# One pack set less on TensorE, and products of two conv tiles added by accumulating transfers

## The chip, the core and the metric

The kernel runs on one core of a Trainium2 chip. Its metric is the device time of one execution in microseconds; before the change three runs gave 802.43, 802.77 and 803.06 us, median 802.77. A core has four engines that compute, each with its own instruction stream: TensorE (PE, matmuls, with its weight loads shown as PEld), VectorE (DVE), ScalarE (ACT) and GpSimd (POOL). SyncE (SP) issues transfers. The engines meet only at semaphores.

## The reference

Two decoder layers over 512 positions of width 1024 in float32: a Conformer convolution layer, then latent attention. The change is in the first one:

```python
proj = h @ w_in + b_in                       # 512 x 1024 @ 1024 x 6144
val, glu_gate, z = jnp.split(proj, 3, axis=-1)
u = val * jax.nn.sigmoid(glu_gate)           # 512 x 2048
u = causal depthwise conv(u, conv_w, 31 taps per channel) + conv_b
u = jax.nn.silu(layer_norm(u, norm_g, norm_b))
return (u * jax.nn.silu(z)) @ w_out + b_out
```

The layer norm is over all 2048 channels, so the mean needs every channel's convolution.

## The kernel before

**Tiles and chunks.** Channels lie on the partitions: the 2048 channels are 16 tiles of 128 partitions x 512 positions. The input projection goes by chunks of 128 output columns: chunks 0 to 31 alternate value and gate (pair t is chunks 2t and 2t+1 and gives tile t of u), chunks 32 to 47 give the 16 tiles of z (z0 to z15). For accuracy a float32 product is three matmuls of high and low parts: with 8 row blocks a chunk is 24 matmuls. For each chunk SyncE loads the weights (w_raw, 512 KB), ScalarE writes the high part (w_hi, L1013), GpSimd the low part (w_lo, L820, a "split"), and TensorE multiplies. There are two buffers of w_raw and four of w_hi and w_lo.

**Pair t on ScalarE** (`value_gate`, L1039): w_hi of both chunks, then val of tile t-1 (waits for TensorE to finish chunk 2t-2), products "before gating", starts of VectorE chains, then the sigmoid of tile t-1 (waits for chunk 2t-1), products "after gating", further starts. On GpSimd (`value_gate`, L835): two splits, product additions, u of tile t-1 (val times sig, L832), more.

**The convolution** is done in three ways.
- *VectorE tiles* (`convolve`, L1518): 12 tiles in the order of VECTOR_TILES, each as two chains of multiply-add in two PSUM banks (L1470), then joined (L1496). ScalarE starts a tile by writing its first taps to the banks (`start_chains`, L1059); where it does so is in the START tables. The last one, LATE_TILE, has its first 17 taps summed elsewhere and 14 here.
- *Shared tiles*: ScalarE multiplies u by one tap into a ring of four buffers (`tap_times_u`, L1083), GpSimd adds it (L860). These are all taps of tile 1 and the first 17 of tile 11.
- *Matrix tiles* 4, 8 and 12 (`pack`, L1941): u is written to DRAM, read back shifted (`stacked`), and four packs of six matmuls follow four chunks of the projection (from PACKS_AT). ScalarE keeps each pack's result, SyncE moves its parts (`move_parts`), and VectorE adds three of them (`add_parts`, L1499).

**After that** VectorE and GpSimd add all 16 tiles to csum; TensorE sums csum over partitions inside chunk z11 (`sum_over_channels`, L1980), VectorE centres the tiles, the squares are summed in z14, and the projection of the branch follows. Every engine's order is written out in the program; the tables below set where each piece stands.

Of the kernel before, what the change touches and what calls it, by code (L numbers as in the profile page):

```python
# [122 lines left out]
def trunk_kernel(nc, x, positions, ln_g, ln_b, a_w_in, a_b_in, a_conv_w, a_conv_b, a_norm_g,  # L123
# [14 lines left out]
    with ExitStack() as ctx:  # L138
# [388 lines left out]

        def pair_taps(t):

            first = sum(n for at_pair, n in PAIR_SHARE.items() if at_pair < t)  # L530
            return range(first, first + PAIR_SHARE.get(t, 0))

        def z_taps(i):

            first = sum(PAIR_SHARE.values()) + sum(n for at_chunk, n in Z_SHARE.items() if at_chunk < i)
# [1731 lines left out]
```

## Time and profile before

| what | value |
|---|---|
| median of three runs | 802.77 us (802.43 to 803.06) |
| the profiled execution | 800.57 us |
| its span, first to last instruction | 798.8 us |
| TensorE busy | 786.2 us, 98% |
| VectorE busy | 587.5 us, 74% |
| GpSimd busy | 527.9 us, 66% |
| ScalarE busy | 392.3 us, 49% |
| granted TensorE clock | 0.999 |

A busy share is an average over stages with different limits: VectorE's 74% hides a stretch of some 240 us in which it never rests. Matmuls overlap in the pipeline, so their busy times add up to more than they cost; the interval from one to the next is what counts. Line numbers in rows are those of the kernel before.

### The profile page before, as it was taken

The numbers are of one execution on the slowest core, as the hardware profiler recorded it, in microseconds if no ns is written. First come the engines' busy times: TensorE is split into PE (matmuls) and PEld (weight loads), VectorE is DVE, ScalarE is ACT, GpSimd is POOL, SyncE is SP. The second block draws the span as 40 slices with busy tenths as digits, with TensorE's granted clock in tenths as the row PEclk, the third lists the DMA queues.
The fourth block names the chain that finished last, engine by engine and source line by source line (L and its number), as shares of the span: only waits on it lengthen the run. The fifth ranks groups of instructions, "written<-read, shape, count | busy, mean of one in ns | idle before, by whom it ended". The sixth has DMA issues, their size and how long they took to land.

```text
span 798.8 us, 11166 instructions
## 1 busy us (share of the span) xinstructions
PE 786.2 (98%) x3811; PEld 664.6 (83%) x3811; DVE 587.5 (74%) x1000; ACT 392.3 (49%) x687; POOL 527.9 (66%) x324
## 2 busy tenths in 40 slices
PE   7999999999999999999999999999999999999996
PEld 7888888888888878888988788889888888888885
DVE  3699999999999869975633490059788988877217
ACT  4555554653734577521433453157676766655110
POOL 4589997996997763862564457247768667367430
PEclk9999999999999999999999999999999999999999
DMA  6333476564653325632333225236666664653412
GB/s 226 106 106 92 129 193 176 133 189 139 157 141 109 103 80 163 208 122 62 106 106 118 80 79 172 66 106 181 188 186 202 191 204 134 197 181 130 158 54 105
DMA packets 130030, 111.35 MB, mean 139 GB/s; under 512 B 16986, under 2 KB 109248, under 8 KB 129980
## 3 DMA queue, kind: packets, MB, share of 16 engines
q1 hardware_dynamic: 129980, 110.72, 47.1%
q8 instruction: 27, 0.44, 0.2%
q14 instruction: 23, 0.19, 0.1%
HBM read 88.85 MB, written 14.25 MB: 129 GB/s over the span
## 4 chain that ended last, share of the span: by engine, by line
PE 86%; POOL 6%; issue 4%; DMA 2%; DVE 0%; SPq 0%; ACT 0%; DVEq 0%; POOLq 0%
PE bank L1867 81%; POOL w_lo L820 5%; PE bank L2180 1%; PE bank L2181 1%; DMA x_in<-in_x_dram 1%; POOL res L936 1%; PE bank L1957 1%; PE bank L1954 1%; PE bank L1955 1%; POOL vsum_odd L885 1%; DMA w_raw<-in_a_w_out_dram 1%; PE bank L2054 0%; PE bank L2173 0%; PE bank L2171 0%; PE bank L2107 0%
## 5 line engine op out<-in xcount | busy, mean ns | idle before, releaser
L820 POOL TENSOR_TENSOR w_lo<-w_raw,w_hi 128x1024 fp32r<-128x1024 f32 x102 | 253.7, 2496 | 122.7 <-ACT w_hi L1013 115.2
L1470 DVE SCALAR_TENSOR_TENSOR bank<-u,conv_w,bank 128x512 f32<-128x512 f32 x291 | 193.6, 748 | 0.0
L1013 ACT ACTIVATE w_hi<-w_raw 128x1024 fp32r<-128x1024 f32 x102 | 107.4, 1057 | 105.5 <-DMA w_raw<-in_a_w_in_dram 43.0
L1867 PE MATMUL bank<-xt_hi,w_lo 128*128 128x512 f32 (+1 forms) x392 | 152.1, 388 | 0.0
L1867 PE MATMUL bank<-xt_hi,w_hi 128*128 128x512 f32 (+1 forms) x392 | 150.9, 385 | 0.0
L1867 PE MATMUL bank<-xt_lo,w_hi 128*128 128x512 f32 (+1 forms) x392 | 150.9, 385 | 0.0
L1867 PEld LDWEIGHTS bank<-xt_lo,w_hi 128*128 128x128 f32 x392 | 73.7, 188 | 15.1 <-issue 0.5
L1867 PEld LDWEIGHTS bank<-xt_hi,w_lo 128*128 128x128 f32 x392 | 73.7, 188 | 15.0 <-issue 0.5
L1867 PEld LDWEIGHTS bank<-xt_hi,w_hi 128*128 128x128 f32 x392 | 73.6, 188 | 14.9
L1867 PE MATMUL bank<-ht_hi,w_lo 128*128 128x512 f32 (+1 forms) x208 | 76.4, 367 | 0.0
L1867 PE MATMUL bank<-ht_lo,w_hi 128*128 128x512 f32 (+1 forms) x208 | 75.8, 365 | 0.0
L1867 PE MATMUL bank<-ht_hi,w_hi 128*128 128x512 f32 (+1 forms) x208 | 75.8, 365 | 0.0
L972 POOL TENSOR_TENSOR pt_lo<-prob_moved,pt_hi 128x512 fp32r<-128x512 f32 (+1 forms) x64 | 55.9, 906 | 17.8 <-ACT pt_hi L1342 17.8
L941 POOL TENSOR_TENSOR bundle_lo<-bundle_raw,bundle_hi 128x1024 fp32r<-128x1024 f32 (+1 forms) x16 | 49.2, 3074 | 27.1 <-ACT bundle_hi L1269 27.1
L860 POOL TENSOR_TENSOR acc<-acc,tap_product 128x512 f32<-128x512 f32 x46 | 59.6, 1296 | 4.1 <-ACT tap_product L1093 0.8
L1867 PE MATMUL bank<-w_hi,fg_lo 128*128 128x512 f32 x128 | 50.1, 391 | 0.7 <-issue 0.7
L1867 PE MATMUL bank<-w_hi,g_lo 128*128 128x512 f32 x128 | 50.2, 392 | 0.6 <-POOL w_lo L820 0.3
L1867 PE MATMUL bank<-w_hi,g_hi 128*128 128x512 f32 x128 | 49.9, 389 | 0.0
L1867 PE MATMUL bank<-w_hi,fg_hi 128*128 128x512 f32 x128 | 49.8, 389 | 0.0
L1867 PE MATMUL bank<-w_lo,fg_hi 128*128 128x512 f32 x128 | 49.8, 389 | 0.0
L1867 PE MATMUL bank<-w_lo,g_hi 128*128 128x512 f32 x128 | 49.8, 389 | 0.0
L1643 DVE SCALAR_TENSOR_TENSOR bank<-res,bank 128x512 f32<-128x512 f32 x16 | 11.0, 689 | 50.4 <-PE bank L1867 50.4
(225 smaller groups left out, 1730.4 us busy)
## 6 DMA issues: line engine op xcount, KB each, us to landing
w_raw<-in_a_w_in_dram SPq DMA_DIRECT2D x48, 512.0 KB, 3.8
w_raw<-in_b_w_in_dram SPq DMA_DIRECT2D x20, 512.0 KB, 3.7
prob_kept<-prob SPq DMA_DIRECT2D x16, 640.0 KB, 3.5
prob_moved<-prob_kept SPq DMA_DIRECT2D x64, 160.0 KB, 3.2
w_raw<-in_a_w_out_dram SPq DMA_DIRECT2D x16, 512.0 KB, 4.0
w_raw<-in_b_w_out_dram SPq DMA_DIRECT2D x16, 512.0 KB, 3.6
stacked<-u_kept SPq DMA_DIRECT2D x48, 132.0 KB, 4.1
bundle_raw<-in_b_w_uq_dram SPq DMA_DIRECT2D x16, 256.0 KB, 4.5
```

The source lines that it names most:

```text
L820: nc.gpsimd.tensor_tensor(w_lo[slot][:], w_raw[raw][:], w_hi[slot][:].bitcast(F32), ALU.subtract).then_inc(w_lo_ready, 1)
L860: nc.gpsimd.tensor_tensor(acc[:, t, :], acc[:, t, :], tap_product[n % 4][:], ALU.add).then_inc(product_added, 1)
L885: nc.gpsimd.tensor_tensor(vsum_odd[:], vsum_odd[:], sq[t % 4][:], ALU.add).then_inc(vsum_odd_done, 1)
L936: nc.gpsimd.tensor_tensor(res[:, r, :], res[:, r, :], ln_rows[:, 2, :], ALU.add).then_inc(res_ready, 1)
L941: nc.gpsimd.tensor_tensor(bundle_lo[slot][part][:], bundle_raw[:, lo:hi], bundle_hi[slot][part][:].bitcast(F32), ALU.subtract).then_inc(bu ...
L972: nc.gpsimd.tensor_tensor(turned_block(pt_lo, b), moved_block(b), turned_block(pt_hi, b).bitcast(F32), ALU.subtract).then_inc(pt_lo_ready, 1)
L1013: nc.scalar.activation(w_hi[slot][:], w_raw[raw][:], ACT.Copy).then_inc(w_hi_ready, 1)
L1470: nc.vector.scalar_tensor_tensor(out=inner[:] if k < TAPS - 1 else acc[:, t, :], in0=u[:, t, k:k + SEQ], scalar=conv_w[:, column:column + ...
L1643: nc.vector.scalar_tensor_tensor(out=total[:], in0=rows_half, scalar=scale, in1=total[:], op0=ALU.mult, op1=ALU.add).then_inc(y_step, 1)
L1867: last = nc.tensor.matmul(out_ap, a, b, start=(start and n == 0 and m == 0), stop=(stop and n == len(parts) - 1 and m == 2))
L1954: nc.tensor.matmul(out[:], matrix_lo[:, g, s, :], stacked[:, 0, g, window], start=s == 0, stop=False)
L1955: nc.tensor.matmul(out[:], matrix_hi[:, g, s, :], stacked[:, 0, g, window], start=False, stop=False)
```

## The change

The tiles are dealt out anew. Matrix tiles are 8 and 12; tile 4 leaves them. BEGINS goes from (6, 10, 14) to (10, 14), PACKS_AT from (17, 25, 35) to (26, 35). Tile 4 becomes the late tile, with 22 taps summed by ScalarE and GpSimd and 9 on VectorE; tile 11 becomes a full VectorE tile and tile 7 a shared one. Most products of tiles 1 and 7 are no longer added one at a time. ScalarE writes four of them side by side (four tiles' width, in parts of acc and z_a that are free then), and GpSimd issues one transfer that adds these 128 x 2048 values to four running sums. There are 11 such transfers; then GpSimd adds the four sums to one. Tile 1 has 7 groups of four (the first is written as the sums) and 3 single taps, tile 7 has 6 groups and 7 single taps. VectorE waits for six and for ten groups before the last tap of tiles 9 and 13, whose places in acc the groups use; ScalarE waits for all 11 before z1.

```diff
-        MATRIX_ROWS = (1, 2, 3)
+        MATRIX_ROWS = (2, 3)
-        BEGINS = (6, 10, 14)
-        PACKS_AT = (17, 25, 35)
+        BEGINS = (10, 14)
+        PACKS_AT = (26, 35)
-        LATE_TILE, LATE_TAPS = 11, 17
-        SHARED_TILES = (1,)
-        VECTOR_TILES = (0, 2, 3, 5, 6, 7, 9, 10, 13, 14, 15, LATE_TILE)
-        PAIR_SHARE = {3: 3, 4: 4, 5: 2, 6: 3, 7: 4, 8: 3, 9: 4, 10: 3, 11: 1, 12: 4, 13: 4, 14: 3, 15: 1}
-        Z_SHARE = {0: 1, 1: 2, 2: 2, 3: 2, 4: 2}
+        GROUPED_TILES = (1, 7)
+        LATE_TILE, LATE_TAPS = 4, 22
+        VECTOR_TILES = (0, 2, 3, 5, 6, 9, 10, 11, 13, 14, 15, LATE_TILE)
+        GROUP = 4
+        FIRST_GROUPS, SECOND_GROUPS = 6, 5
+        GROUP_PAIRS = (4, 5, 6, 7, 8, 9, 11, 12, 13, 14, 15)
...
+        for t, n in ((6, 3), (7, 2), (8, 2), (9, 3), (12, 3), (13, 4), (14, 2), (15, 1)):
+            AFTER_GATING[t] = taps_of(LATE_TILE, first, n)
+            first += n
+        IN_Z[1] = taps_of(LATE_TILE, first, LATE_TAPS - first)
+        first = GROUPED_TAPS[1]
+        for i, n in ((3, 2), (4, 2), (5, 2), (6, 1)):
+            IN_Z[i] = taps_of(LATER, first, n)
+            first += n
...
-        PARTS_AFTER = {7: 0, 13: 1, LATE_TILE: 2}
+        PARTS_AFTER = {13: 0, LATE_TILE: 1}
-        START_BEFORE_GATING = {5: 3, 7: 5, 10: 7, 15: 13}
-        START_AFTER_GATING = {3: 2, 8: 6, 11: 9, 13: 10}
-        START_IN_Z = {1: 14, 7: 15, 10: LATE_TILE}
+        START_BEFORE_GATING = {5: 3, 7: 5, 11: 9, 12: 10, 14: 11, 15: 13}
+        START_AFTER_GATING = {3: 2, 8: 6}
+        START_IN_Z = {3: 14, 7: 15, 10: LATE_TILE}
...
+                if t == GROUP_PAIRS[FIRST_GROUPS]:
+                    sum_group(0)
+                if t == GROUP_PAIRS[FIRST_GROUPS] + 1:
+                    add_products(BEFORE_GATING[10])
+                add_products(AFTER_GATING.get(t - 1, ()))
                 if t > 0:
                     glu(t - 1, (t - 1) % 2)
+                if t in GROUP_PAIRS:
+                    add_group(GROUP_PAIRS.index(t))
...
+            def add_group(g):
+
+                t, k = BEFORE_GATING[GROUP_PAIRS[g]][-1]
+                pool.wait_ge(product_ready, shared_taps.index((t, k)) + 1)
+                wait(pool, group_added, 16 * g)
+                nc.gpsimd.dma_start(group_sums(t)[:], group_products(g)[:], accum_op=ALU.add).then_inc(group_added, 16)
+
+            def sum_group(which):
+
+                t = GROUPED_TILES[which]
+                pool.wait_ge(group_added, 16 * (FIRST_GROUPS + which * SECOND_GROUPS))
+                for n in range(1, GROUP):
...
+                elif apart(t, k):
+                    g = k // GROUP - 1 + FIRST_GROUPS * GROUPED_TILES.index(t)
+                    wait(act, group_added, 16 * (g - 1))
+                    if g == 7:
+                        act.wait_ge(group_summed, GROUP - 1)
+                    out = group_products(g)[:, k % GROUP, :]
...
+                if i == 1:
+                    act.wait_ge(group_added, 16 * len(GROUP_PAIRS))
...
+                    if t in (9, 13) and k == TAPS - 1:
+                        dve.wait_ge(group_added, 16 * (FIRST_GROUPS if t == 9 else 10))
```

Three places show how this moves instructions. The first is GpSimd in pair 14 and the start of pair 15; L820 (before) and L858 (after) are splits, L832 and L870 write u. Before:

```order
L820 TENSOR_TENSOR w_lo0_77<-w_raw0_71,w_hi0_73 128x1024
L820 TENSOR_TENSOR w_lo1_78<-w_raw1_72,w_hi1_74 128x1024
L860 TENSOR_TENSOR acc_105<-acc_105,tap_product3_120 128x512
L860 TENSOR_TENSOR acc_105<-acc_105,tap_product0_117 128x512
L860 TENSOR_TENSOR acc_105<-acc_105,tap_product1_118 128x512
L832 TENSOR_TENSOR u_95<-val1_83,sig1_85 128x512
L877 TENSOR_TENSOR u_lo_96<-u_95,cu_hi_86 128x542
L820 TENSOR_TENSOR w_lo2_79<-w_raw0_71,w_hi2_75 128x1024
L820 TENSOR_TENSOR w_lo3_80<-w_raw1_72,w_hi3_76 128x1024
L860 TENSOR_TENSOR acc_105<-acc_105,tap_product2_119 128x512
```

The same stretch on GpSimd after the change:

```order
L858 TENSOR_TENSOR w_lo0_77<-w_raw0_71,w_hi0_73 128x1024
L858 TENSOR_TENSOR w_lo1_78<-w_raw1_72,w_hi1_74 128x1024
L920 TENSOR_TENSOR acc_106<-acc_106,tap_product0_118 128x512
L920 TENSOR_TENSOR acc_106<-acc_106,tap_product1_119 128x512
L920 TENSOR_TENSOR acc_106<-acc_106,tap_product2_120 128x512
L920 TENSOR_TENSOR acc_106<-acc_106,tap_product3_121 128x512
L870 TENSOR_TENSOR u_95<-val1_83,sig1_85 128x512
L899 DMA second_sums_97<-acc_106 128x2048
L937 TENSOR_TENSOR u_lo_96<-u_95,cu_hi_86 128x542
L858 TENSOR_TENSOR w_lo2_79<-w_raw0_71,w_hi2_75 128x1024
L858 TENSOR_TENSOR w_lo3_80<-w_raw1_72,w_hi3_76 128x1024
L920 TENSOR_TENSOR acc_106<-acc_106,tap_product0_118 128x512
```

This pair has one addition more, all ahead of u, and the transfer stands between u and u_lo.

The second place is ScalarE where it starts VectorE's sixth tile, in banks 3 and 7. Before, this is pair 10 and tile 7:

```order
L1013 ACTIVATE w_hi0_73<-w_raw0_71 128x1024
L1036 ACTIVATE part_out0_108<-bank6 128x512
L1013 ACTIVATE w_hi1_74<-w_raw1_72 128x1024
L1019 ACTIVATE val1_83<-bank0,vec_51 128x512
L1093 ACTIVATE tap_product3_120<-u_95,conv_w_62 128x512
L1093 ACTIVATE tap_product0_117<-u_95,conv_w_62 128x512
L1093 ACTIVATE tap_product1_118<-u_95,conv_w_62 128x512
L1069 ACTIVATE bank3<-u_95,vec_51,conv_w_62 128x512
L1072 ACTIVATE bank7<-u_95,conv_w_62 128x512
```

After the change it is tile 9, from the end of pair 10 into pair 11:

```order
L1176 ACTIVATE cu_hi_86<-u_95 128x542
L1169 ACTIVATE second_sums_97<-u_95,vec_51,conv_w_62 128x512
L1171 ACTIVATE second_sums_97<-u_95,conv_w_62 128x512 x3
L1077 ACTIVATE w_hi2_75<-w_raw0_71 128x1024
L1077 ACTIVATE w_hi3_76<-w_raw1_72 128x1024
L1083 ACTIVATE val0_82<-bank2,vec_51 128x512
L1171 ACTIVATE z_a_111<-u_95,conv_w_62 128x512 x4
L1131 ACTIVATE bank3<-u_95,vec_51,conv_w_62 128x512
L1134 ACTIVATE bank7<-u_95,conv_w_62 128x512
```

The start of the sixth tile has moved back by one pair, behind the val of tile 10 and four products.

The third place is VectorE from the late tile to csum. Before:

```order
L1481 SCALAR_TENSOR_TENSOR bank<-u,conv_w,acc 128x512
L1470 SCALAR_TENSOR_TENSOR bank<-u,conv_w,bank 128x512 x10
L1470 SCALAR_TENSOR_TENSOR acc<-u,conv_w,bank 128x512
L1470 SCALAR_TENSOR_TENSOR bank<-u,conv_w,bank 128x512
L1496 TENSOR_TENSOR acc<-bank,acc 128x512
L1507 TENSOR_TENSOR bank<-u,bank 128x508
```

VectorE at the same place after the change:

```order
L1562 SCALAR_TENSOR_TENSOR bank<-u,conv_w,acc 128x512
L1551 SCALAR_TENSOR_TENSOR bank<-u,conv_w,bank 128x512 x4
L1551 SCALAR_TENSOR_TENSOR acc<-u,conv_w,bank 128x512
L1551 SCALAR_TENSOR_TENSOR bank<-u,conv_w,bank 128x512 x2
L1577 TENSOR_TENSOR acc<-bank,acc 128x512
L1588 TENSOR_TENSOR bank<-u,bank 128x508
```

Five multiply-adds are gone, and the last two of the first chain now follow each other.

## Rows read from the trace of the kernel before

**Rows 1.** The page, part 1: busy time of each engine.
```profile
PE 786.2 (98%) x3811; PEld 664.6 (83%) x3811; DVE 587.5 (74%) x1000; ACT 392.3 (49%) x687; POOL 527.9 (66%) x324
```
**Rows 2.** Waits of PE: who waited, for whom, us in total, times, longest.
```profile
PE bank L1885 <- DMA x_in<-in_x_dram: 2.7, 3, 2.4
...
PE bank L1867 <- POOL w_lo L820: 0.3, 1, 0.3
PE bank L1867 <- DVE g_lo L1595: 0.2, 1, 0.2
```
**Rows 3.** The chain that ended last: start us, us, what.
```profile
168.67 5.45 PE bank L1867 x24
175.52 5.45 PE bank L1867 x24
...
221.85 5.44 PE bank L1867 x24
```
**Rows 4.** Timeline at the mean: start us, us, engine, line, operation.
```profile
263.41 0.68 DVE L1507 TENSOR_TENSOR bank<-u,bank 128x508 f32<-128x508 f32 x1
...
265.46 0.69 DVE L1456 COPY bank<-acc 128x512 f32<-128x512 f32 x1
...
267.05 0.69 DVE L1458 TENSOR_TENSOR csum<-bank,pool_csum 128x512 f32<-128x512 f32 x1
...
267.86 0.39 PEld L1983 LDWEIGHTS bank<-csum,ones 128*128 128x128 f32 x2
```
**Rows 5.** Stretches: busy us of PE, PEld, DVE, ACT, POOL; clock, DMA share, GB/s.
```profile
30.00:90.00 60.00, 60.00 (x266) 49.66 (x265) 59.74 (x94) 32.60 (x49) 53.31 (x32) 1.00 0.36 106
90.00:150.00 60.00, 60.00 (x266) 49.56 (x265) 59.90 (x91) 33.11 (x48) 53.89 (x34) 1.00 0.58 159
```
**Rows 6.** Timeline of DVE: the fifth and sixth tile, and the late tile's first tap.
```profile
110.37 17.86 DVE L1470 SCALAR_TENSOR_TENSOR bank<-u,conv_w,bank 128x512 f32<-128x512 f32 x27
...
130.20 17.87 DVE L1470 SCALAR_TENSOR_TENSOR bank<-u,conv_w,bank 128x512 f32<-128x512 f32 x27
...
253.25 1.62 DVE L1481 SCALAR_TENSOR_TENSOR bank<-u,conv_w,acc 128x512 f32<-128x512 f32 x1
```
**Rows 7.** Timeline of ACT in pairs 6 to 12.
```profile
78.76 0.69 ACT L1025 ACTIVATE sig<-bank,vec 128x512 f32<-128x512 f32 x1 [2.86 <-PE bank L1867]
79.34 0.65 ACT L1099 ACTIVATE cu_hi<-u 128x542 fp32r<-128x542 f32 x1
...
84.84 2.55 ACT L1093 ACTIVATE tap_product<-u,conv_w 128x512 f32<-128x512 f32 x4
87.30 0.77 ACT L1069 ACTIVATE bank<-u,vec,conv_w 128x512 f32<-128x512 f32 x1
...
100.52 0.69 ACT L1025 ACTIVATE sig<-bank,vec 128x512 f32<-128x512 f32 x1 [2.85 <-PE bank L1867]
...
140.66 2.00 ACT L1013 ACTIVATE w_hi<-w_raw 128x1024 fp32r<-128x1024 f32 x2
```
**Rows 8.** Timeline of POOL in pairs 11, 12, 14, 15 and at z3.
```profile
111.42 4.18 POOL L860 TENSOR_TENSOR acc<-acc,tap_product 128x512 f32<-128x512 f32 x3
115.56 1.29 POOL L832 TENSOR_TENSOR u<-val,sig 128x512 f32<-128x512 f32 x1
...
128.18 1.38 POOL L877 TENSOR_TENSOR u_lo<-u,cu_hi 128x542 fp32r<-128x542 f32 x1
...
177.51 4.75 POOL L820 TENSOR_TENSOR w_lo<-w_raw,w_hi 128x1024 fp32r<-128x1024 f32 x2
...
189.89 1.99 POOL L871 TENSOR_TENSOR matrix_hi<-same_channel,stack_hi 128x1024 fp32r<-128x1024 f32 x1
...
210.42 2.42 POOL L820 TENSOR_TENSOR w_lo<-w_raw,w_hi 128x1024 fp32r<-128x1024 f32 x1
```
**Rows 9.** One more stretch, columns as in rows 5.
```profile
150.00:207.00 57.00, 57.00 (x253) 47.07 (x252) 56.86 (x88) 31.42 (x46) 49.47 (x31) 1.00 0.64 170
```
**Rows 10.** SyncE's issue of a load (timeline), and the landing of loads (page, part 6).
```profile
231.83 0.53 SPq L566 DMA_DIRECT2D w_raw<-in_a_w_in_dram  x1
...
w_raw<-in_a_w_in_dram SPq DMA_DIRECT2D x48, 512.0 KB, 3.8
```

More of the change, by code:

```diff
@@ L419, in added_before, with taps_of @@
-        def added_before(n):
-            return sum(1 for _, k in shared_taps[:n] if k > 0)
+        GROUPED_TILES = (1, 7)
[4 more added lines that the diff above has]
+        GROUP_PAIRS = (4, 5, 6, 7, 8, 9, 11, 12, 13, 14, 15)
+        GROUPED_TAPS = (GROUP * (FIRST_GROUPS + 1), GROUP * (SECOND_GROUPS + 1))
+        def taps_of(t, first, n):
+            return [(t, k) for k in range(first, first + n)]
@@ new lines, in trunk_kernel @@
+        first = 0
+        for t, n in ((6, 3), (7, 2), (8, 2), (9, 3), (12, 3), (13, 4), (14, 2), (15, 1)):
[6 more added lines that the diff above has]
+            first += n
+        shared_taps = [tap for t in range(CT) for half in (BEFORE_GATING, AFTER_GATING) for tap in half.get(t, ())]
@@ new lines, in trunk_kernel, with apart, added, added_up_to @@
+        shared_taps += [tap for i in range(CT) for tap in IN_Z.get(i, ())]
+        def apart(t, k):
+            return t in GROUPED_TILES and k < GROUPED_TAPS[GROUPED_TILES.index(t)]
+        def added(t, k):
+            return k > 0 and not apart(t, k)
+        def added_up_to(tap):
+            return sum(1 for t, k in shared_taps[:shared_taps.index(tap) + 1] if added(t, k))
+        def group_sums(t):
+            return acc[:, CT - GROUP:, :] if t == EARLIER else second_sums
+        def group_products(g):
+            if g in (7, 9):
+                return acc[:, CT - GROUP:, :]
+            if g in (1, 3, 5):
+                return acc[:, CT - 2 * GROUP:CT - GROUP, :]
+            return z_a[:, 1:1 + GROUP, :]
@@ L526, in starts_before @@
             return 2 * STARTED.index(t) + (0 if t == LATE_TILE else slot)
[L528 to L535, printed above, removed]
-            return range(min(first, len(shared_taps)), min(first + Z_SHARE.get(i, 0), len(shared_taps)))
         LOOP_BEGINS, LOOP_ROUNDS = 3, 2
@@ new lines, in add_products @@
+            def add_products(taps):
+                for t, k in taps:
+                    if not added(t, k):
+                        continue
+                    if t in GROUPED_TILES:
+                        pool.wait_ge(group_summed, (GROUP - 1) * (GROUPED_TILES.index(t) + 1))
+                    pool.wait_ge(product_ready, shared_taps.index((t, k)) + 1)
+                    wait(pool, product_added, added_up_to((t, k)) - 1)
+                    nc.gpsimd.tensor_tensor(acc[:, t, :], acc[:, t, :], tap_product[added_up_to((t, k)) % 4][:], ALU.add
+                                            ).then_inc(product_added, 1)
@@ L910, in _ @@
                     split_lo(Z0 + 1, 1, 1)
+                    add_products(AFTER_GATING[CT - 1])
                     glu(CT - 1, (CT - 1) % 2)
-                for n in z_taps(i):
-                    add_product(n)
+                if i == 2:
+                    sum_group(1)
+                add_products(IN_Z.get(i, ()))
                 if i >= POOL_SUM_BEGINS:
@@ L1043, in value_gate @@
                 keep_value(t - 1, (t - 1) % ROUND)
-                for n in pair_taps(t)[:BEFORE_GATING + 1]:
-                    tap_times_u(n)
-                if t in PARTS_START_IN_PAIR:
-                    start_parts(PARTS_START_IN_PAIR[t])
+                for tap in BEFORE_GATING.get(t, ()):
+                    tap_times_u(*tap)
                 if t in START_BEFORE_GATING:
@@ L1053, in value_gate @@
                     conv_input_hi(BEGINS.index(t))
-                for n in pair_taps(t)[BEFORE_GATING + 1:]:
-                    tap_times_u(n)
+                for tap in AFTER_GATING.get(t, ()):
+                    tap_times_u(*tap)
                 if t in START_AFTER_GATING:
@@ L1199, in _ @@
                     square(t)
-                for n in z_taps(i):
-                    tap_times_u(n)
+                for tap in IN_Z.get(i, ()):
+                    tap_times_u(*tap)
             output_split(0)
```

79 lines of the change are left out of this document (46 added, 33 removed).

## The prediction

> **What bounds the kernel now.** I read the page first: TensorE is busy 98% of the span [rows 1]. The table of waits, filtered to TensorE, says the same from the other side: its longest in total is 2.7 us, at the start for x, and for the other engines' work it waits 0.3 and 0.2 us in the whole run [rows 2]. So any matmul that goes is worth its issue interval, as long as nobody comes late to a place where TensorE asks for something. The chain of waits gives that interval: 24 matmuls of a chunk take 5.44 us (0.227 each), and with a pack behind the chunk the next starts 6.85 us later, so a pack of six costs 1.40 us [rows 3]. Not 6 x 0.39: busy times of matmuls overlap.
>
> The next view is the timeline around the mean over channels, in chunk z11. VectorE writes csum, 267.05 to 267.74; TensorE's weight load for the sum starts at 267.86, in step with its own rhythm [rows 4]. VectorE has been busy without a gap since 30 us (59.7 of 60, 59.9 of 60) [rows 5]. At this place two engines bound the kernel together: TensorE's gain counts only as far as VectorE comes earlier too. What follows the mean (centring, variance, projection) is the same code, started by csum, so I take its length as unchanged.
>
> **The change, part by part.**
>
> *TensorE.* One pack set of three goes: 4 packs x 1.40 = 5.6 us. Without any wait TensorE would ask for csum at 267.86 - 5.6 = 262.3.
>
> *VectorE, removed.* The late tile takes 9 taps for 14, one of each begun by ScalarE. 27 taps take 17.86 us, 0.66 each [rows 6]: 5 x 0.66 = 3.3, less some 0.1 because the order now ends with two dependent taps (x2 in the listing). One set of three part additions goes: 263.41 to 265.46, 2.05 us [rows 4]. The first late tap stays at its 1.62 us [rows 6]. Together -5.25 us: csum at 262.5, nearly as early as TensorE.
>
> *VectorE, a new wait.* VectorE's sixth tile starts when ScalarE has put its first tap into the banks. Before, tile 7 was started in pair 10; now it is tile 9, in pair 11, behind four grouped products. VectorE is free at 130.20 [rows 6]; the starts of the tiles before it keep their places or have some 2 us of room. ScalarE's sigmoid of tile 5 is at 78.76 and of tile 7 at 100.52 [rows 7], which is 4 chunks x 5.44. No pack now stands behind chunks 17 to 20, so the end of chunk 20 comes at 100.52 + 5 x 5.44 = 127.7. ScalarE reaches it from the sigmoid of tile 9 (122.3) with 0.6 for that, 0.55 for cu_hi, 2.6 for the four products of tile 7, 2.0 for two w_hi [rows 7]: 128.0. Then val 0.6, four products 2.46 (84.84 to 87.30), the start 0.77: 131.8. VectorE stands still 131.8 - 130.2 = 1.6 us. It has no later slack: it never idles before csum. The other starts have room. A tile lasts 19.8 us (110.37 to 130.20) [rows 6], so VectorE wants tile 10 at 131.8 + 19.8 = 151.6; ScalarE starts it after val of tile 11 (end of chunk 22, 138.6) and 4.5 us more, at 143.1. Tile 11 is wanted at 171.4 and started near 166 (end of chunk 26, 160.4).
> csum then comes at 267.74 - 5.25 + 1.6 = 264.1, TensorE waits about 1.8 us for it, and the gain is 3.65 us, say 3.7.
>
> *GpSimd.* 46 additions become 37, and 11 accumulating transfers are issued. From pair 10 on GpSimd is the busiest after VectorE, and TensorE needs its w_lo. Intervals [rows 8]: split 2.37, addition 1.37 (three 4.14), u 1.24, u_lo 1.32, the two matrices 3.9. Let X be GpSimd's time for one transfer. If u of tile 8 waits for its sigmoid (112.1), it ends at 113.4. Then: one X; pair 10, 2 splits, 3 additions, u, u_lo 11.4; pairs 11 to 13, 10.1 + X each; pair 14 with four additions and u_lo 12.8 + X; pair 15 with two additions and the matrices 12.6 + X; split of z0 2.4. Sum 182.9 + 6X. TensorE begins z0 at 100.52 + 16 x 5.44 + 4 x 1.40 = 193.2. So GpSimd is in time up to X = 1.7. Above that, pairs 8 and 9 lose their slack too (counted from u of tile 6: sigmoid of tile 5 at 78.76, three products and a w_hi to 82.2, two splits and two additions to 89.7, the sigmoid it waits for at 90.3, done at 91.6; then 8.7 + X for each of the two pairs and their X), and z0 is late by 8X - 14.6. A lateness under 1.8 costs nothing, since TensorE would wait for csum anyway. The next tight place is z3, where three additions of tile 7's sums lie ahead: before, its split was done at 212.84 [rows 8], and z4 began at 221.85 [rows 3], so z3 at 221.85 - 1.40 - 5.44 = 215.0: 2.2 us early. With X = 1.3 I get about the same: u of tile 15 ends at 195.1, two additions, a split, three additions and a split later it is 206.8 for 209.4. From z5 on there are four additions more, but GpSimd has rest there once ScalarE waits for the last pack.
>
> What is X? No row shows a transfer issued by GpSimd. From below SyncE's issue, 0.53 us [rows 10]; from above the time in which GpSimd itself works through as many columns, two splits, 4.75 us. I take 1.3, between, nearer to SyncE's row because the instruction only names the data. At 1.3 z0 is ready 2.4 us early and the cost is 0.
> The Trainium skill ("DMA: Bandwidth & Descriptors", section on latency and other measured facts) gives about 1 us for the first byte on the GpSimd path; no run here shows it so far. By it the sum would be the same 3.7.
>
> *The transfers.* Each adds 1 MB to 1 MB in SBUF. GpSimd waits before each for the one before, issued 10.9 us or more earlier. Bounds for the landing: 3.8 us, as a 512 KB load takes [rows 10], and 11.4, three times that, since 3 MB move (two reads, a write) for 1 MB. I take 7.6, two loads' worth: no wait. The DMA engines are already busy 0.36, 0.58 and 0.64 of three stretches [rows 5, 9]; the weight loads would land later, and they have some 3.6 us of room (split to split of a slot 10.9, less split 2.4, load 3.8, w_hi 1.05).
> The Trainium skill (same page, section on issuing engines that are not separate DMA queues) says that all transfers share the same 16 engines whoever issues them. That speaks against the change; its own fit (2.0 us plus size over 436 GB/s, section on the anatomy of one DMA) gives 4.4 us as an estimate for 1 MB, and then nothing is late.
>
> *ScalarE.* 36 more products at 0.62 = 22 us in a stretch where it is busy 33 of 60 us. They delay no w_hi that GpSimd is waiting for, except through the ring of four products in pairs 13 and 14, where I see about 1 us of room. Taken as 0. The first pack in z waits for VectorE's parts of tile 8, done at 131.8 + 4 x 19.8 + 2.05 = 213.1; TensorE comes there at 215.0 - 5.6 + 5.44 = 214.8.
>
> **Sum.** -5.6 + 1.8 (wait for csum) = -3.7 us with rounding. Against the profiled execution (800.57 us, of it 798.8 span) that is 796.9; it lies 2.2 under the median of the runs, 802.77, on which I forecast 799.1.
>
> **Rivals.**
> 1. *TensorE's whole gain.* The start of tile 9 is in time, or VectorE catches up: -5.25 to -5.6, 797.3. For it: the stall rests on 1.6 us of ScalarE's order. Against: the order is fixed, and VectorE has no gap to catch up in.
> 2. *GpSimd late, but not by more than the packs were worth.* X between 2.0 and 2.5: z0 late by 1.8 to 5.4, result 799.1 to 802.6. For and against as in rival 3.
> 3. *Slower: GpSimd's issue.* w_lo of z0 is the place. From X = 2.5 the lateness passes 5.6. At X = 3, 8 x 3 - 14.6 = 9.4, less 5.6: 3.8 slower, 806.6. For it: 4.75 us is not excluded, and GpSimd works 53.9 of 60 us there [rows 5]. Against: SyncE's 0.53.
> 4. *Transfers land late.* GpSimd then stands before the next one. With landing time L, from the transfer of pair 7 at 91.6: two L to that of pair 9, 22.9 through pair 10 to that of pair 11, four L to that of pair 15, 7.6 to z0's w_lo. That is 122.1 + 6L, late from L = 11.9, slower from 12.8; at 13 the lateness is 6.9 and the result 804.1, at 14 810. For it: an upper bound of 11.4 and shared engines; against: the lower ones.
> That the set of packs doesn't go is excluded: the listing has eight packs.
>
> **Numbers.** Forecast 42%; rival 1 12%; rival 2 16% (6 faster, 10 within); rival 3 18%; rival 4 12%, both counted slower. So faster by over 0.2% (1.6 us, about what a measurement of this kernel can tell from no change) 60%, within 10%, slower 30%. The likeliest case alone spans 798.3 to 800.0. The range for 8 in 10 takes in rival 1 and about two thirds of 3 and 4: 796.8 to 806.
>
> **What the profile after would show.** Right: 16 matmuls of each pack line; VectorE idle about 1.6 us before its sixth tile, with ScalarE's start as releaser; TensorE idle near 1.8 us before the csum product and nowhere else before it; GpSimd's splits in time at z0 and z3. Wrong: TensorE waiting for w_lo in pairs 12 to 15 or z0 (X too small), GpSimd idle ahead of a transfer (landing), ScalarE waiting longer for weight loads, or no wait at csum (rival 1).

## The result: 0.39% slower

| | median | lowest to highest | profiled execution | its span |
|---|---|---|---|---|
| before | 800.77 us | 799.16 to 803.35 us, and one run of 2050.48 us | 800.57 us | 798.8 us |
| after | 803.60 us | 801.03 to 807.09 us | 802.84 us | 801.0 us |

The ratio is 1.0039, with a 95% interval from 1.0027 to 1.0052 (20 runs of each, the one of 2050.48 us left out): some 3 us slower, where 3.7 us less was forecast (799.1 on a median of 802.77, a ratio of 0.9954). The forecast was reckoned from three runs; twenty put the kernel before at 800.77. The measured time lies inside the range that was given, 796.8 to 806, on the other side of no change. The runs of after also scatter over 6 us.

**TensorE.** The table of waits of the kernel after, from 100 to 215 us (who waited, for whom, us in total, times, longest):

```profile
ACT w_hi L1077 <- DMA w_raw<-in_a_w_in_dram: 15.6, 8, 3.6
...
PE bank L2035 <- ACT part_out L1100: 4.4, 1, 4.4
DVE bank L1551 <- ACT bank L1131: 2.1, 1, 2.1
```

Before, TensorE's waits for other engines' work were 0.2 and 0.3 us in the whole run [rows 2]. Now there is one of 4.4 us at a pack's first matmul (L2035), for ScalarE's copy of the preceding pack's result (L1100). VectorE's new wait, forecast at 1.6 us, is there with 2.1. The chain that ended last, of after, says why ScalarE was late (start, us, what):

```profile
148.69 2.71 POOL w_lo L858
151.47 0.39 SPq L602
151.90 0.70 SPq L619
...
155.61 0.86 SPq L619
156.58 8.10 DMA w_raw<-in_a_w_in_dram
164.93 0.74 issue
165.67 0.67 ACT val L1083
...
166.85 1.94 ACT acc L1171 x3
168.78 0.67 ACT bank L1131
169.45 0.61 ACT bank L1134
170.07 0.53 ACT part_out L1100
170.73 0.77 PE bank L2035
...
172.77 0.85 PE bank L2038 x2
173.63 6.71 PE bank L1948 x24
```

Read from the bottom: the pack began at 170.73 because ScalarE's copy of the pack before came at 170.07; ahead of it in ScalarE's order stand a start (L1131, L1134), four grouped products and val; and val stands behind w_hi of chunk 29, whose weights took 8.1 us to land. SyncE issued that load behind four shifted reads of tile 8 (L619) that took 4.58 us to issue; in kernel 9 below, which has no transfers, they took 2.00.

The same rows hold a second cost. The late pack takes 173.63 - 170.73 = 2.90 us where 1.40 is normal, and the chunk behind it 6.71 for 5.44 [rows 3]: 2.8 us more, with nobody waiting. The stretches of after show it (busy us of PE, PEld, DVE, ACT, POOL; granted clock, DMA share, GB/s):

```profile
160.00:163.00 3.00, 3.00 (x14) 2.46 (x14) 3.00 (x6) 1.31 (x2) 2.29 (x3) 1.00 1.17 221
...
166.00:169.00 3.00, 0.35 (x2) 0.00 (x0) 3.00 (x6) 3.00 (x6) 3.00 (x2) 1.00 0.97 224
169.00:172.00 3.00, 1.27 (x3) 1.11 (x4) 2.97 (x6) 3.00 (x6) 2.71 (x3) 0.55 0.36 105
172.00:175.00 3.00, 3.00 (x8) 2.32 (x8) 3.00 (x6) 2.35 (x4) 2.86 (x4) 0.50 0.46 112
175.00:178.00 3.00, 3.00 (x12) 2.38 (x12) 3.00 (x6) 0.66 (x1) 3.00 (x3) 0.81 1.06 296
```

After TensorE had stood, the granted clock was at its lower level (0.50, 1.2 GHz) while it worked again, 8 matmuls in 3 us for 15 in the same 3 us before, and back at 1.00 behind 178.

**The mean.** Timeline of after from VectorE's last steps to csum and TensorE's product (start, us, engine, line, operation, idle time before and its releaser):

```profile
262.44 0.70 DVE L1537 TENSOR_TENSOR bank<-bank,acc 128x512 f32<-128x512 f32 x1
264.07 0.69 DVE L1537 TENSOR_TENSOR csum<-bank,pool_csum 128x512 f32<-128x512 f32 x1 [0.94 <-POOL pool_csum L965]
...
268.84 1.02 PE L2064 MATMUL bank<-csum,ones 128*128 128x512 f32 x2
```

csum was done at 264.76, where 264.1 was forecast, but TensorE came 4 us later: 268.84, before 268.06. Since its first matmul of the projection was 0.76 us earlier in after (11.03 for 11.79: x landed sooner), the sum up to here is -5.6 (packs) + 4.4 (standing) + 2.8 (clock) = +1.6, and the traces say 268.84 - 268.06 + 0.76 = +1.5. From this product to the end of the span it is 532.2 us against 530.7, +1.4 more, at the same code. In total -0.8 + 1.5 + 1.4 = 2.2 with rounding, the difference of the spans.

**The transfers.** Queues and issues, page of after, parts 3 and 6 (packets, MB, share of 16 engines; KB each, median us to landing):

```profile
q0 software_dynamic: 1584, 11.54, 7.5%
...
w_raw<-in_a_w_in_dram SPq DMA_DIRECT2D x48, 512.0 KB, 4.1
stacked<-u_kept SPq DMA_DIRECT2D x32, 132.0 KB, 6.1
acc<-z_a POOLq DMA_DIRECT2D x3, 1024.0 KB, 7.3
...
second_sums<-acc POOLq DMA_DIRECT2D x2, 1024.0 KB, 9.4
```

q0 is GpSimd's queue: 7.5% of 801 us is 60 us of all 16 engines, 5.5 us for each of eleven transfers. From 150 to 170 us the DMA share is 1.07, where before it was 0.70. A short stretch above 1 stood in before too (1.06 from 160 to 163 us); what is new is how long it lasts, 1.03 over 137 to 169 us for 0.61. The shifted reads land in 6.1 us instead of 4.1 (medians, as all landings of this table). GpSimd's issue is short, and what comes right behind it is some 0.3 us longer (two splits, 5.07 for 4.75):

```profile
137.03 0.87 POOL L899 DMA_DIRECT2D second_sums<-z_a  x1
137.64 5.07 POOL L858 TENSOR_TENSOR w_lo<-w_raw,w_hi 128x1024 fp32r<-128x1024 f32 x2
```

### The profile page after: what moved, and what is told of

Read it like the earlier page. It is cut to its first block, busy times and chain, and to the rows that moved or that the text cites. A ratio compares the mean times of both kernels' runs of the same rounds, so it can differ in the third digit from the quotient of the medians.

```text
span 801.0 us, 11092 instructions
## 1 busy us (share of the span) xinstructions
PE 784.1 (98%) x3787; PEld 662.6 (83%) x3787; DVE 575.4 (72%) x992; ACT 410.7 (51%) x717; POOL 523.6 (65%) x323
## 4 chain that ended last, share of the span: by engine, by line
PE 89%; DMA 3%; POOL 2%; SPq 2%; ACT 1%; issue 1%; DVE 1%; DVEq 0%; ACTq 0%
PE bank L1948 84%; POOL pt_lo L1036 1%; DMA w_raw<-in_a_w_in_dram 1%; DMA x_in<-in_x_dram 1%; DMA prob_kept<-prob 1%; PE bank L2261 1%; PE bank L2262 1%; POOL w_lo L858 1%; SPq L619 1%; PE bank L2035 0%; DMA prob_moved<-prob_kept 0%; PE bank L2038 0%; PE bank L2036 0%; POOL bundle_lo L1005 0%; PE bank L2135 0%
## 5 line engine op out<-in xcount | busy, mean ns | idle before, releaser
L858 POOL TENSOR_TENSOR w_lo<-w_raw,w_hi 128x1024 fp32r<-128x1024 f32 x102 | 254.1, 2513 | 127.7 <-ACT w_hi L1077 120.2
L1551 DVE SCALAR_TENSOR_TENSOR bank<-u,conv_w,bank 128x512 f32<-128x512 f32 x286 | 190.4, 748 | 2.2 <-ACT bank L1131 2.1
L1948 PE MATMUL bank<-xt_hi,w_lo 128*128 128x512 f32 (+1 forms) x392 | 152.6, 389 | 0.0
L1948 PE MATMUL bank<-xt_hi,w_hi 128*128 128x512 f32 (+1 forms) x392 | 151.4, 386 | 0.0
L1948 PE MATMUL bank<-xt_lo,w_hi 128*128 128x512 f32 (+1 forms) x392 | 151.3, 386 | 0.0
L1948 PEld LDWEIGHTS bank<-xt_hi,w_lo 128*128 128x128 f32 x392 | 74.1, 189 | 15.2 <-issue 0.5
L1948 PEld LDWEIGHTS bank<-xt_lo,w_hi 128*128 128x128 f32 x392 | 74.0, 189 | 15.2 <-issue 0.5
L1948 PEld LDWEIGHTS bank<-xt_hi,w_hi 128*128 128x128 f32 x392 | 73.9, 189 | 14.9
L1948 PE MATMUL bank<-ht_hi,w_lo 128*128 128x512 f32 (+1 forms) x208 | 76.4, 367 | 1.0 <-DVE ht_lo L1758 1.0
L1948 PE MATMUL bank<-ht_lo,w_hi 128*128 128x512 f32 (+1 forms) x208 | 75.8, 365 | 0.0
L1948 PE MATMUL bank<-ht_hi,w_hi 128*128 128x512 f32 (+1 forms) x208 | 75.8, 365 | 0.0
L1036 POOL TENSOR_TENSOR pt_lo<-prob_moved,pt_hi 128x512 fp32r<-128x512 f32 (+1 forms) x64 | 60.2, 975 | 16.3 <-ACT pt_hi L1421 16.3
L1948 PE MATMUL bank<-w_hi,fg_lo 128*128 128x512 f32 x128 | 50.1, 391 | 0.7 <-issue 0.7
L1948 PE MATMUL bank<-w_hi,g_lo 128*128 128x512 f32 x128 | 50.0, 391 | 0.2 <-DVE g_lo L1676 0.2
L1948 PE MATMUL bank<-w_hi,g_hi 128*128 128x512 f32 x128 | 49.8, 389 | 0.0
L1948 PE MATMUL bank<-w_lo,g_hi 128*128 128x512 f32 x128 | 49.8, 389 | 0.0
L1948 PE MATMUL bank<-w_hi,fg_hi 128*128 128x512 f32 x128 | 49.8, 389 | 0.0
L1948 PE MATMUL bank<-w_lo,fg_hi 128*128 128x512 f32 x128 | 49.8, 389 | 0.0
L1948 PEld LDWEIGHTS bank<-ht_hi,w_lo 128*128 128x128 f32 x208 | 39.2, 189 | 7.6 <-DVE ht_lo L1758 1.2
```

What stands on the lines that cost most here:

```text
L858: nc.gpsimd.tensor_tensor(w_lo[slot][:], w_raw[raw][:], w_hi[slot][:].bitcast(F32), ALU.subtract).then_inc(w_lo_ready, 1)
L1036: nc.gpsimd.tensor_tensor(turned_block(pt_lo, b), moved_block(b), turned_block(pt_hi, b).bitcast(F32), ALU.subtract).then_inc(pt_lo_ready, 1)
L1551: nc.vector.scalar_tensor_tensor(out=inner[:] if k < TAPS - 1 else acc[:, t, :], in0=u[:, t, k:k + SEQ], scalar=conv_w[:, column:column + ...
L1948: last = nc.tensor.matmul(out_ap, a, b, start=(start and n == 0 and m == 0), stop=(stop and n == len(parts) - 1 and m == 2))
```

## The experiments

All are the changed kernel with the edit shown, unless said otherwise; ratios are to the kernel before on the same chip, with 95% intervals.

**1. The pack's result is kept first** (`keep_first`).

```diff
                 keep_value(t - 1, (t - 1) % ROUND)
+                keep_pack_after(2 * t - 2)
                 for tap in BEFORE_GATING.get(t, ()):
                     tap_times_u(*tap)
                 if t in START_BEFORE_GATING:
                     start_chains(START_BEFORE_GATING[t])
-                keep_pack_after(2 * t - 2)
```

> The changed kernel with one thing moved: ScalarE keeps a pack's result ahead of the four products and the start of a VectorE tile, not behind them (pairs 14 and 15). Theory T: the result of the sign is one stall. TensorE waited 4.4 us at the second pack of tile 8 for ScalarE to keep the first pack's result, and its clock then fell, which cost some 3.3 us more (34 matmuls fewer than in before between 150 and 190 us, 34 x 0.227 = 7.7, of it 4.4 standing). ScalarE was late because a weight load landed late and because products and a start (4.0 us) stood ahead of the keep. With the keep first the stall is at most 0.5 us, the clock stays at 1.00, TensorE comes to the csum product at 269.0 - 7.7 = 261.3 and waits there for VectorE's csum (264.8, or 263.8 without its 0.9 us wait for GpSimd). Time some 4.2 to 5 us below the changed kernel, about 799 against 803.6, 0.2% to 0.3% under the kernel before. Rival R (the loss is spread: slower loads and GpSimd's issues everywhere, the stall is only where it shows): the stall turns up at another place, and the time stays within 1.5 us of the changed kernel, 0.2% to 0.4% over the kernel before.

Measured 1.0021 (1.0000 to 1.0042), where the change had 1.0039: 1.4 us gained, not 4.2 to 5, and the two intervals overlap. The stall at the packs went from 4.4 to 1.4 us, but TensorE reached the csum product at 268.57, hardly earlier. Its waits from 100 to 215 us:

```profile
PE bank L1948 <- issue: 2.9, 2, 1.8
PE bank L2035 <- ACT part_out L1100: 1.4, 2, 0.9
```

The chain of this kernel puts the new ones at 199.63 and 206.41, ahead of z chunks (L1948), where tile 12's shifted reads run and w_hi waited up to 6.1 us for a load; the stretches from 206 to 214 us show a clock of 0.89 and 0.68. In after, TensorE did not stand there (20.00 of 20 us busy from 190 to 210, at a DMA share of 0.98): its stall at 166 had put it behind. So T was right on the place and wrong on the cause: not one stall but a shortage, and rival R came nearer.

**2. Kept ahead of the start only** (`keep_mid`): in the diff above the line stands between the products and the start.

> The changed kernel with the keep of a pack's result moved only ahead of the start of a VectorE tile (1.4 us of the 4.0), behind the four products. Asks for the price of a stall by its length. Theory T: the stall falls from 4.4 to about 3.0 us and the clock still falls, at the same extra of about 3.3: TensorE at the csum product near 267.6, time 1.4 us below the changed kernel. Rival (the extra goes with the length of the stall): 4.4 to 3.0 takes 7.7 to 5.2, 2.5 us below.

Measured 1.0023 (1.0007 to 1.0039). TensorE stood 3.1 us. Its chain shows what that cost in clock:

```profile
169.18 0.69 PE bank L2035
...
171.15 0.85 PE bank L2038 x2
172.00 5.86 PE bank L1948 x24
```

2.82 us for the pack and 5.86 for the chunk, 1.4 + 0.4 = 1.8 us too much, against 2.8 after a stall of 4.4 us. The extra is not fixed. With 1.3 us less standing the csum product came 2.5 us earlier, at 266.37, of which 0.3 is an earlier first matmul: the expectation's rival came nearer. The medians of the runs gained 1.3 us, which the intervals do not tell from none.

**3. And tile 9 started first** (`keep_start9`): as 1, and for t == 11 the start stands ahead of the products.

> As the kernel with the keep first, and in pair 11 ScalarE starts tile 9 ahead of the four products of tile 7. Theory T: VectorE's 2.1 us wait before its sixth tile goes, csum is 1 to 2 us earlier than in the kernel with the keep first (as far as GpSimd's own sum is in time), TensorE waits less at the mean, and the time falls by another 1 to 2 us, to about 797.5, 0.4% under the kernel before. If GpSimd's sum is the later one, the gain stays under 0.5 us. Rival R: no difference, since VectorE is not what the end waits for.

Measured 1.0024 (1.0004 to 1.0044), as kernel 1. VectorE still waited 1.5 us for the start (val ahead of it was late) and 2.4 us for GpSimd's sum, and then 5.0 us for TensorE. Where TensorE is late, an earlier csum is worth nothing.

**4. Small transfers** (`small_transfers`).

```diff
-                nc.gpsimd.dma_start(group_sums(t)[:], group_products(g)[:], accum_op=ALU.add)
+                nc.gpsimd.dma_start(group_sums(t)[:, :, 0:32], group_products(g)[:, :, 0:32], accum_op=ALU.add)
```

> The changed kernel with each accumulating transfer cut to 32 of its 512 columns: the issue on GpSimd, ScalarE's products, every wait and SyncE's order stay, what the DMA engines move is a sixteenth. The other columns of the groups' sums are left out. Theory T (the DMA engines were full from 137 to 169 us and made the load late): loads land in 3.8 us as before, the stall goes from 4.4 to under 1 us, DMA share in 150 to 170 falls from 1.07 to about 0.7, the time is that of the kernel with the keep first, about 799. Rival S (SyncE's queue: the load's issue stands behind four shifted reads whatever the engines do): the load's issue still comes at about 156.6 and the stall keeps 2 us or more. Rival A (ScalarE's 22 us more of products by themselves make it late): the stall stays 3 us or more, the time within 1 us of the changed kernel.

Measured 0.9977 (0.9961 to 0.9992), 799.0 us: T's number. Stall 1.5 us at the pack, clock in 150 to 210 us 1.00, csum product at 263.57:

```profile
150.00:170.00 20.00, 18.46 (x82) 14.98 (x81) 19.96 (x32) 16.40 (x26) 19.31 (x12) 1.00 0.53 120
170.00:190.00 20.00, 20.00 (x90) 16.47 (x89) 19.96 (x31) 11.38 (x17) 19.82 (x13) 1.00 0.71 172
```

ScalarE's products, all waits and SyncE's order are the same, so what the DMA engines moved made the loss. Rival S holds for a part, though: the load of chunk 29 was still issued at 155.94 us (156.58 in after, 152.89 without any transfers), behind four reads whose issue took 3.30 us, and w_hi of that chunk began at 161.66 for 159.12 without transfers; the 1.5 us of standing come with that. Nor is GpSimd's own issue the same: it takes 1.28 us for such a cut transfer and 0.87 for a whole one. In the time none of this shows, since TensorE would have waited for csum anyway (kernel 9).

**5. Only tile 7's transfers small** (`second_small`): the same cut for g >= 6.

> As the kernel with small transfers, but only the five of tile 7 (pairs 11 to 15) are cut to 32 of 512 columns, the six of tile 1 (pairs 4 to 9) stay whole; the other columns of tile 7's group sums are left out. Theory T2 (from the first four runs: the loss comes where accumulating transfers meet the shifted reads and the part moves of the packs, and keeping the result earlier only lets the next late load strike, at 199 and 206 us): the same time as with all transfers small, 799.0, since in pairs 4 to 9 the transfers meet nothing but the loads. Rival (every whole transfer costs a little, 1 MB each): six of eleven whole, so about half way, 801.5.

Measured 0.9969 (0.9959 to 0.9979). The six whole transfers in pairs 4 to 9 cost nothing that the runs can tell, though the DMA share from 30 to 90 us is 0.63 for 0.43, and 0.84 for 0.42 from 90 to 120 us; the loss comes from the five in pairs 11 to 15, among the packs' reads and moves.

**6. The reads of tile 8 earlier** (`stack_early`), and **7. with the edits of 3** (`stack_early_keep`).

```diff
-        BEGINS = (10, 14)
+        BEGINS = (9, 14)
...
-                    elif 5 <= n < 5 + PACKS:
-                        stack_u(m, n - 5)
+                    elif 5 - (m == 0) <= n < 5 - (m == 0) + PACKS:
+                        stack_u(m, n - 5 + (m == 0))
```

> The changed kernel with the shifted reads of tile 8 moved from 144 to 157 us into the gap between the transfers of pairs 9 and 11, about 119 to 137 us: u of tile 8 is written to DRAM a pair earlier and its reads are issued three chunks earlier. All transfers are whole. Theory T2: the loads of chunks 28 and 29 meet one transfer, not a transfer and sixteen reads; they land 2 us or more earlier, and the stall at the second pack falls from 4.4 to about 1.5 us, as with small transfers, with no fall of the clock. The crowd of tile 12's reads (189 to 210 us) is still there and may then strike, 2 to 3 us. Time 1 to 4 us below the changed kernel, so 799.5 to 802.5. Rival (SyncE's queue and ScalarE's order set it, not what the engines move): no change, 803.6.

> The same early reads, with the pack's result kept first and tile 9 started first as in the third run. Aims at a version that is faster than both. Theory T2: the stall at the second pack goes (it rested on the late load and on ScalarE's order), and TensorE meets the second crowd as early as in the kernel with the keep first: if that still costs 2.9 us standing and a fall of the clock the time is 802; if the earlier work on GpSimd and SyncE leaves room there it is 798 to 799.

Measured 1.0044 (1.0026 to 1.0061) and 1.0002 (0.9990 to 1.0014). In kernel 6 the stall at the second pack fell to 1.5 us and the clock held, as expected, and the time did not fall: VectorE now waited 6.1 us before its sixth tile, and TensorE 1.9 us for w_hi in the second crowd.

```profile
PE bank L1948 <- ACT w_hi L1077: 1.9, 1, 1.9
PE bank L2035 <- ACT part_out L1100: 1.5, 1, 1.5
```

The reads moved the shortage to 119 to 137 us, where the DMA share is 0.81 for 0.60 in after. Kernel 7, with both of ScalarE's orders mended, was level with the kernel before.

**8. Ten groups** (`ten_groups_early`, on kernel 7; `ten_groups`, on kernel 3): the transfer of pair 15 goes.

```diff
-        FIRST_GROUPS, SECOND_GROUPS = 6, 5
-        GROUP_PAIRS = (4, 5, 6, 7, 8, 9, 11, 12, 13, 14, 15)
+        FIRST_GROUPS, SECOND_GROUPS = 6, 4
+        GROUP_PAIRS = (4, 5, 6, 7, 8, 9, 11, 12, 13, 14)
...
-        for t, n in ((6, 3), (7, 2), (8, 2), (9, 3), (12, 3), (13, 4), (14, 2), (15, 1)):
+        for t, n in ((6, 3), (7, 3), (8, 3), (9, 3), (12, 3), (13, 4), (14, 2), (15, 1)):
...
-        for i, n in ((3, 2), (4, 2), (5, 2), (6, 1)):
+        for i, n in ((3, 3), (4, 3), (5, 3), (6, 2)):
```

> The early reads of tile 8, the pack's result kept first, tile 9 started first, and the transfer of pair 15 taken out: four taps of tile 7 go from a group to single additions in z3 to z6, and two taps of the late tile move from z1 to pairs 7 and 8, where GpSimd has rest. Nothing is left out of the result. Theory T2 (loss only where a transfer meets the packs' reads): the last crowd, 184 to 206 us, loses its transfer, the load that ScalarE waited 7.3 us for lands in time, and TensorE no longer stands 3.3 us there. csum is then VectorE's, near 263.5 (its tile 9 is still started 1 to 2.7 us late), or GpSimd's, whose chain of additions from 200 to 262 us grows by 2.7 us: 264 to 265. Time 798 to 799.5, 0.2% to 0.3% under the kernel before. Rival (the crowd is SyncE's order of reads, moves and loads): the stall stays, time 801.

> The same with the reads of tile 8 where the change has them (144 to 157 us), among the transfers of pairs 12 and 13. Theory T2: the load of chunk 29 is late as before, the keep comes early enough, some 1.3 us of standing at the packs remain, and the second crowd is relieved: 799.5 to 801, worse than with the early reads by about 1 us.

Measured 1.0009 (0.9998 to 1.0021) and 1.0007 (0.9990 to 1.0025): no gain over the kernel before, so neither reached its forecast, and no version with all its transfers whole beat the kernel before. The stall in 190 to 210 us did go (PE busy 20.00 of 20 in both traces). With the early reads VectorE waited 4.8 us before its sixth tile and TensorE then 2.8 us for csum; without them the packs stood 2.7 us.

**9. No transfers** (`no_transfers`), and **10. with tile 9 started first** (`no_transfers_start9`).

```diff
-                nc.gpsimd.dma_start(group_sums(t)[:], group_products(g)[:], accum_op=ALU.add)
+                nc.gpsimd.tensor_tensor(group_sums(t)[:, :, 0:8], group_sums(t)[:, :, 0:8], group_products(g)[:, :, 0:8], ALU.add)
```

> The changed kernel with each accumulating transfer replaced by a GpSimd addition of 8 of the 512 columns; the rest of the groups' sums is left out. No DMA is issued by GpSimd at all. Beside the kernel with small transfers it prices the issue: eleven issues of 0.87 us against eleven tiny additions. Theory T2: GpSimd is not what the end waits for, so the time is that of the small transfers, 799.0. Theory Q (a program that has GpSimd's DMA queue pays for it later: the 64-column load at 383 us takes 4.1 us for 3.3 in every kernel with the change): that load lands in 3.3 us again, the stretch after the mean is back at 529.7 us, and the time is 797.2.

> The kernel without transfers (GpSimd adds 8 of 512 columns in their place), and ScalarE starts tile 9 ahead of the four products in pair 11. There TensorE waited 1.6 us for VectorE's csum and nowhere else. Theory T (the prediction's step: VectorE has no slack, so its 2.1 us wait before the sixth tile comes out at csum): VectorE's wait falls under 0.5 us, TensorE's at csum goes from 1.6 to 0, and the time falls by 1.5 us, from 0.9977 to 0.9958 of the kernel before, 797.1. Rival (GpSimd's own sum or the late tile's products then end last): TensorE still waits 1 us or more, the gain is under 0.6 us.

Measured 0.9977 (0.9966 to 0.9988) and 0.9949 (0.9931 to 0.9967). In kernel 9 TensorE waited for an engine at one place ahead of the mean, the one that the prediction named (1.8 us there):

```profile
263.60 1.10 PE L2064 MATMUL bank<-csum,ones 128*128 128x512 f32 x2 [1.56 <-DVE csum L1537]
```

In kernel 10 this wait is gone, VectorE's before its sixth tile too, and the product starts at 262.29, 1.3 us earlier; the time came out at 0.9949 where 0.9958 was expected.

Kernel 9 also shows how late the transfers made ScalarE in after, where w_hi of chunk 29 begins at 164.70 and the copy at 170.00 (its timeline, start, us, what):

```profile
159.12 1.06 ACT L1077 ACTIVATE w_hi<-w_raw 128x1024 fp32r<-128x1024 f32 x1 [0.63 <-DMA w_raw<-in_a_w_in_dram]
...
164.45 0.58 ACT L1100 ACTIVATE part_out<-bank 128x512 f32<-128x512 f32 x1
```

Here the load of chunk 29 is issued at 152.89 and takes 6.2 us. So of the 5.6 us by which it is late in after, 3.7 lie in its issue (156.58) and 1.9 in its landing (8.1).

**11. What lengthens the stretch after the mean.** `before_q0` is the kernel before with one plain transfer by GpSimd at its start; `before_dram1` and `after_dram1` keep u in one DRAM tensor of the same size in both kernels; `dram3` gives the changed kernel a third, unused one.

```diff
+            nc.gpsimd.dma_start(z_a[:, 5, 0:8], ones[:, 0:8]).then_inc(q0_used, 16)
+            pool.wait_ge(q0_used, 16)
```

```diff
-        u_kept = [nc.dram_tensor(f"u_kept{m}", [2, P, SEQ + PAD], F32).ap() for m in range(3)]
+        u_kept = nc.dram_tensor("u_kept", [4, 2, P, SEQ + PAD], F32).ap()
```

> The changed kernel with a third, unused DRAM tensor beside the two for u, as the kernel before had. Asks why the stretch after the mean is 1.4 to 2.5 us longer in all five traces with the change than in before (798.8 - 269.1 = 529.7 against 531.1 to 532.2), though its code is the same: the load of the 64-column weight lands 0.8 to 0.9 us later (4.1 for 3.3) and TensorE then waits 1.0 us at 391. Theory P (place in DRAM): with the third tensor the load lands in 3.3 us, the wait goes, and the time falls by about 1 us, to 802.6. Rival N (chance or something that the first stretch leaves behind): the load takes 4.1 again and the time stays at 803.6.

> The kernel before with one plain transfer of 8 columns issued by GpSimd at its start, into a place that is written again later. Theory Q: the mere use of GpSimd's queue lengthens the 64-column load to 4.1 us and the time by 1 to 2 us, 802. Rival N (the short tail of the one profile of the kernel before was chance, or comes from the time at which that stretch starts): the time is that of before within 0.1%, 800.7.

> The kernel before with its three DRAM tensors for u made one, a third larger. Theory P (what follows lies elsewhere in DRAM): the 64-column load takes 4.1 us as in the kernels with the change, TensorE stands 1 us there, and the time rises by 1 us, to 801.6. Rival N (the change in the first stretch is what matters): 3.1 to 3.3 us, time unchanged, 800.6.

> The changed kernel with its two DRAM tensors for u made one of that same size. Theory P: the load takes what it takes in the kernel before with the same tensor, whichever that is. Rival N: 4.1 us, and 3.1 to 3.3 in the other. The stall at the second pack stays in both cases, time 803 to 805.

Measured, in the order of the expectations: dram3 1.0071 (1.0056 to 1.0085), before_q0 1.0012 (1.0000 to 1.0024), before_dram1 0.9991 (0.9979 to 1.0002) and after_dram1 1.0028 (1.0015 to 1.0040). The 64-column load near 384 us, from its DMA view, in the kernel before with one tensor and in the changed one with the same:

```profile
w_raw<-in_kv_w_down_dram SPq DMA_DIRECT2D x2, 256.0 KB, 3.1
```

```profile
w_raw<-in_kv_w_down_dram SPq DMA_DIRECT2D x2, 256.0 KB, 4.2
```

It is 3.1 to 3.3 us in the three traces of kernels with the first stretch of before, and 3.8 to 4.2 in all with that of after, those without any transfer too. From the csum product to the end of the span it is 530.7 to 531.3 us in the same three traces and 532.0 to 533.9 in all others. So it is neither the use of GpSimd's queue, nor the accumulating transfers, nor the DRAM layout that was varied. What it is stays open. dram3 was slower than after ahead of the mean as well (5.2 us standing at the pack), which its edit doesn't explain.

## Why the prediction was wrong, point by point

- **TensorE, -5.6 us**: right. With no transfers and tile 9 first, the way from the first matmul of the projection to the csum product is (268.06 - 11.79) - (262.29 - 11.32) = 5.3 us shorter than before, VectorE's 5.25.
- **VectorE, -5.25 and a new wait of 1.6**: right (2.1 measured; csum at 264.76 for 264.1, of it 0.9 for GpSimd's sum, which I had not counted). Kernels 9 and 10 show the wait passing through to TensorE: it stands 1.6 us for csum in 9, and in 10 its product comes 1.3 us earlier.
- **GpSimd's issue X, 1.3 us**: too large, 0.87, with some 0.3 behind it. Up to the mean TensorE never waited for w_lo in after, as said. Rivals 2 and 3 fall.
- **Landing, 7.6 us**: near, medians of 7.3 to 9.4. GpSimd never stood before a transfer, so rival 4 in its own form falls too, and with it the sign that I had named for it: the transfers cost without anyone waiting for them. The other sign, ScalarE waiting longer for weight loads, is not in the sums either: 15.6 us from 100 to 215 us, before 18.2. There was no wait at csum, a sign that I had given to rival 1, and the kernel was slower.
- **"The weight loads would land later, and they have some 3.6 us of room"** is the step that failed. The path that I counted this room on, load, w_hi, split, did hold: TensorE never waited for w_lo. But the room was not 3.6 us everywhere. ScalarE's copy of a pack's result stands behind the same w_hi, and there it was 1.3 us: done at 165.03 in kernel 9, asked for by TensorE at 166.35 in after (170.73 - 4.38). The load of chunk 29 was 5.6 us late, and 5.6 - 1.3 is the stall of 4.4 us, with rounding. What I did not work out is how late a load gets. I had put down a landing of 7.6 us and a share of 0.64 side by side and never added them: a transfer every 11 us or so that holds all 16 engines for 5.5 us, as measured since, adds about 0.5 to 0.64, and that is over 1. The Trainium skill ("DMA: Bandwidth & Descriptors", issuing engines that are not separate DMA queues), cited in the prediction as speaking against the change, says that whoever issues, the 16 engines are the same; experiments 4, 5 and 9 agree with it (0.9977, 0.9969 and 0.9977, against 1.0039).
- **"ScalarE: cost 0"** failed with it. I followed w_hi and the ring of four, not the copy of a pack's result. With PACKS_AT moved to an even chunk the first pack's copy stands behind val, four products and a start, 4.3 us of work (165.67 to 170.00), and TensorE asks for it one chunk later. Before, the copy that the third pack waits for stood behind val and three products; it was done at 170.40 us and asked for at 173.96; with tile 4's packs gone and tile 8's begun a chunk later, TensorE comes there 7.6 us earlier (166.35), ScalarE, without transfers, only 5.4. Kernel 9 is just in time, with no stall.
- **The clock** was no term of my sum: 4.4 us of standing cost 2.8 us more.
- **"What follows the mean ... I take its length as unchanged"**: wrong by 1.4 us, cause open.

The sum as it came: -5.6 + 4.4 + 2.8 + 1.4, less 0.8 us at x. Without transfers, in kernel 9, the way to the csum product was 3.9 us shorter than before, where 3.7 was forecast, and 1.4 us of that were lost again behind the mean; the runs show 1.8 us (0.9977), half of the forecast. That 799.1 would even so have nearly been met (798.3) would have been luck: it was reckoned from 802.77, 2 us above what twenty runs show.

## What to carry to other kernels

Work moved from an engine to DMA is paid for in DMA-engine time: add its busy share, stretch by stretch, to the share already there, and where the sum passes 1 for long expect loads, and the issues queued with them, to be late, however short the issue and however patient the waiter. In this kernel 0.84 over 30 us cost nothing and 1.03 over 32 us cost the gain; the runs do not say where between them it begins. Look there for what stands behind a load in the order of the engine that receives it, and count with a stall of TensorE what its clock costs behind it: here 1.8 us for 3.1 and 2.8 for 4.4. Mending one place of a shortage moves it to the next: reordering ScalarE and SyncE brought this kernel level with the one before at best (1.0002), while a smaller load on the DMA engines gave 0.9969, in a kernel that leaves out most of tile 7's group sums.

## What the runs showed of the hardware

- An accumulating transfer of 1 MB from SBUF to SBUF held the 16 DMA engines for 5.5 us and landed in 7.3 to 9.4 us (medians of the four forms); its issue took GpSimd 0.87 us. Cut to 64 KB, 32 of every 512 columns, it has 528 packets for 144, and its issue took 1.28 us.
- The load of chunk 29 (512 KB) took 6.2 us to land among tile 8's shifted reads alone and 8.1 us with the transfers as well; the median of all such loads was 3.8 us.
- The granted clock fell to 0.50 behind a stall of 4.4 us and stayed at 1.00 behind one of 1.5 us. The pack and the chunk behind it took 2.8 us too long after 4.4 us of standing, 1.8 after 3.1, and again 2.8 after the 5.2 of dram3. In kernel 1 TensorE stood 1.05 us at 199.63 and 1.80 us at 206.41, and its clock was 0.89 from 206 to 210 and 0.68 from 210 to 214.
